# Attention beside a paged cache: the key banks' places in the order of steps are moved

## The reference

```python
def nsa_attend(q, qpos, kc, vc, ks_blk, vs_blk, kw, vw, kwpos, gate_logits, rel_bias):
    ...                                  # compressed branch: p_c, o_c, and the importance of each block
    top_val, top_idx = lax.top_k(score, min(TOP_BLOCKS, nb))
    k_sel = gather(ks_blk, top_idx)
    v_sel = gather(vs_blk, top_idx)
    ...
    s_s = einsum('bgrtd,..->bgrtj', qg, k_sel) * scale + bias_s
    p_s = masked_softmax(s_s, mask_s)
    o_s = einsum('bgrtj,..->btgrd', p_s, v_sel)
    ...
    s_w = jnp.einsum('btgrd,bsgd->bgrts', qg, kw) * scale + bias_w
    p_w = masked_softmax(s_w, mask_w)
    o_w = jnp.einsum('bgrts,bsgd->btgrd', p_w, vw)
    return (gts[:, :, 0] * o_c + gts[:, :, 1] * o_s + gts[:, :, 2] * o_w).reshape(b, t, NSA_Q)

def nsa_sample(x, cache_cmp, cache_slc, win_state, page_table, ...):
    ...
    fs = full_rows(cache_slc, kv_s)      # cache[page_table], with the new row behind it
    kw_all = jnp.concatenate([win_state, kv_w], axis=1)
    o = nsa_attend(q, qpos, kc, vc, ks_blk, vs_blk, kw_all[:, :, 0], kw_all[:, :, 1], kwpos, gl, rel_bias)
    return o @ w_out, kv_c, kv_s, kw_all[:, t:]
```

## Time and profile before

| | us |
|---|---|
| three runs | 1723.29, 1721.01, 1731.25 (median 1723.29) |
| the profiled execution | 1718.65 |
| its span, first to last instruction | 1717.0 |
| PE busy (matmul) | 1614.6, 94% |
| VectorE, ScalarE, GpSimd busy | 808.6, 551.0, 564.8 |
| attention, first score product to the last step's | 274.44 to 482.61 |

### The profile page before, as it was taken

How to read it: one execution, slowest core, us unless ns; L and a number is a source line. 1 busy time by engine, 2 the same in 40 slices (tenths; PEclk the granted TensorE clock), 3 DMA queues, 4 the chain that set the end, 5 groups by cost and what they waited for, 6 DMA issues and landing times. The chain is left out here.

```text
span 1717.0 us, 40632 instructions
## 1 busy us (share of the span) xinstructions
PE 1614.6 (94%) x16686; PEld 1502.3 (87%) x16686; DVE 808.6 (47%) x1350; ACT 551.0 (32%) x1040; POOL 564.8 (33%) x505
## 2 busy tenths in 40 slices
PE   6998997798989999999999899999989999999996
PEld 5998985555669999999999889989889999999995
DVE  4333114556555543444237676766447444343235
ACT  3110003456554322222235433333344222222242
POOL 0001222567633433443104333333014444343013
PEclk9999778899999999999999899999989999999998
DMA  9654687777752122223234234433221222223242
GB/s 285 211 187 178 217 293 276 287 239 228 218 193 79 59 88 87 97 86 119 89 132 145 83 113 96 141 111 100 75 89 60 76 96 86 97 86 118 94 160 84
DMA packets 86264, 238.50 MB, mean 139 GB/s; under 512 B 18109, under 2 KB 20847, under 8 KB 84545
## 3 DMA queue, kind: packets, MB, share of 16 engines
q1 hardware_dynamic: 80786, 221.63, 39.2%
q0 software_dynamic: 3392, 11.02, 1.8%
q10 hardware_dynamic: 1936, 3.74, 0.6%
HBM read 217.81 MB, written 23.77 MB: 141 GB/s over the span
## 5 line engine op out<-in xcount | busy, mean ns | idle before, releaser
L846 DVE TENSOR_TENSOR layer_w_lo<-ring,layer_w_hi 128x1024 fp32r<-128x1024 f32 (+1 forms) x138 | 225.5, 1634 | 265.8 <-ACT layer_w_hi L728 265.8
L993 PE MATMUL layer_ps<-layer_x_hi,layer_w_hi 128*128 128x260 f32 x1312 | 269.0, 284 | 2.7 <-DVE layer_w_lo L846 2.7
L993 PE MATMUL layer_ps<-layer_x_hi,layer_w_lo 128*128 128x260 f32 x1312 | 268.3, 284 | 0.0
L993 PE MATMUL layer_ps<-layer_x_lo,layer_w_hi 128*128 128x260 f32 x1312 | 267.8, 284 | 0.0
L728 ACT ACTIVATE layer_w_hi<-ring 128x1024 fp32r<-128x1024 f32 (+1 forms) x138 | 160.9, 1167 | 221.8 <-PE layer_ps L993 206.4
L993 PE MATMUL layer_ps<-layer_h_lo,layer_w_hi 128*128 128x260 f32 x960 | 217.6, 287 | 10.9 <-DVE layer_h_lo L852 10.9
L993 PEld LDWEIGHTS layer_ps<-layer_x_hi,layer_w_hi 128*128 128x128 f32 x1312 | 204.6, 189 | 4.3 <-DVE layer_w_lo L846 2.9
L993 PEld LDWEIGHTS layer_ps<-layer_x_hi,layer_w_lo 128*128 128x128 f32 x1312 | 204.7, 189 | 0.0
L993 PEld LDWEIGHTS layer_ps<-layer_x_lo,layer_w_hi 128*128 128x128 f32 x1312 | 204.0, 189 | 0.1
L993 PE MATMUL layer_ps<-layer_h_hi,layer_w_hi 128*128 128x260 f32 x704 | 172.8, 286 | 4.8 <-DVE layer_w_lo L846 4.8
L993 PEld LDWEIGHTS layer_ps<-layer_h_lo,layer_w_hi 128*128 128x128 f32 x960 | 160.8, 192 | 12.0 <-DVE layer_w_lo L846 11.8
(11 more groups left out here) (319 smaller groups left out, 3055.0 us busy)
## 6 DMA issues: line engine op xcount, KB each, us to landing
ring<-in_w_gu SPq DMA_DIRECT2D x88, 512.0 KB, 3.5
ring<-in_w_down SPq DMA_DIRECT2D x48, 704.0 KB, 4.1
arena<-in_cache_cmp SPq DMA_DIRECT2D x86, 256.0 KB, 5.1
ring<-in_hgrn_w_in SPq DMA_DIRECT2D x32, 512.0 KB, 3.7
X<-in_slc_kv SPq DMA_DIRECT2D x48, 256.0 KB, 3.3
ring<-in_nsa_w_in SPq DMA_DIRECT2D x21, 512.0 KB, 3.7
arena<-in_cache_cmp POOLq DMA_DIRECT2D x42, 256.0 KB, 5.5
ring<-in_slc_kv SPq DMA_DIRECT2D x40, 256.0 KB, 3.0
```

Of the source, the lines that this page charges most:

```text
L846: dve.tensor_tensor(self.w_lo[slot][:, 0:kcs * P], c.ring[:, s, 0:kcs * P], self.w_hi[slot][:, 0:kcs * P].bitcast(F32), ALU.subtract).then ...
L993: mm = pe.matmul(bank[:, h, 0:TH], wt[slot][:, a], xt[:, x, COLS[h]], start=start and part == 0, stop=stop and part == 2)
```

## The change

The four window banks get the turns 0, 3, 6 and 9. The first page bank gets 12 instead of 9, and the page banks follow each other by 2.2 steps instead of 2.45 before the rounding, which moves a turn away from steps of tile 3. The turns of the pages become 12, 15, 16, 18, 21, 24, 25, 27, 30, 31, 34, 36, 39, 40, 42, 45. Every operation of a bank moves with its turn; what the program does, and how often, stays.

```diff
 def bank_turns():
 
-    turns = [0, 1, 3, 6]
+    turns = [0, 3, 6, 9]
     for k in range(SLC_BANKS):
-        t = max(turns[-1] + 1, int(9 + 2.45 * k))
+        t = max(turns[-1] + 1, int(12 + 2.2 * k))
         turns.append(t + (t % 3 == 2))
     return turns
```

## The result

The changed kernel takes 1738.94 us (median of 15 runs, 1730.16 to 1743.56) where the kernel before takes 1723.29 (15 runs too): a ratio of 1.0088, with a 95% interval of 1.0070 to 1.0106. It is slower by 15.65 us. The forecast was +9.5.

The account below looks back on a forecast made before the run. It took TensorE, busy 94% of the span, as the bound, with attention running alone. Attention's first two parts -10.8, third +21.3, end -1.0 make +9.5 us: 1732.8 from a median of 1723.29, range 1713 to 1745.

Parts of the forecast that it names:

- third rival: Attention's early steps: no clock comes back and bank 3 stays 3 us late, so 5 us less gain: 1738; chance 0.1.
- steps 0 to 10: Early attention: less bank work, no window bank waits, one mix wait fewer and some clock back; -14.3 us.
- steps 11 to 19: Attention's second part: PE waits for bank 6, then bank 7 follows late, giving back +3.5 us.
- steps 20 to 46: Late attention: denser steps, nine page banks waited for (18.55 us) and 3.4 of clock; +21.3 us.
- from step 47 on: Attention's end: bank 18's mix leaves step 47, -1.0 us; the rest comes where it came.
- Bank 6's wait: Step 17: PE waits 4 to 5 us for bank 6, whose load stands behind the save of window 3.
- part 3: Attention's steps 20 to 46, 110.85 us before, predicted 132.15, with 3.4 for the clock.
- the nine named: Page banks 8, 10 to 13, 15 and 17 to 19 in steps 20 to 46: waits of 18.55 us in sum.
- The time from mix to scores: Page bank loads: from the mix that frees a slot until the new bank's scores can start, 11.75 us (11.3 to 12.5).
- the loads keep up: Rival: PE finds every page bank of steps 20 to 46 in time, -12.4 us, 1711 on the median's scale; chance 0.2.
- issue loop plus 2.7 for the last transfer: Page bank loads: SP issues eight transfers one by one in 8.02 to 9.06 us; the last lands about 2.7 later.
- Of the clock: Rival: all nine waits of steps 20 to 46 drop the clock, 1.7 us each, +11.9: 1745; chance 0.15.

Follow-up runs that it names:

- Experiment 4: The changed kernel with the window banks back at turns 0, 1, 3, 6 and the page banks as changed: 1745.89 us, ratio 1.0136.
- after: The profiled execution of the changed kernel, with no further edit against it: 1741.56 us.
- Experiments 2: The kernel before the change, with SP reading a bank's eight page numbers before it waits for the slot: 1714.02 us, ratio 0.9949.
- experiment 6: The changed kernel with page numbers read ahead and only the key half of every page transferred: 1711.31 us, ratio 0.9935.
- experiment 7: The changed kernel with window 3 saved earlier and page numbers read ahead, for two banks at once where loads follow closely: 1715.86 us, ratio 0.9974.

## Why the prediction was right, and where its sum was off

The direction, the mechanism and the range held; the sum, +9.5 for +15.65, fell short by 6. The total alone wouldn't have shown the mechanism: 1738.94 is nearer to the 1738 of the prediction's third rival, no early gain, than to the forecast's 1732.8. The steps and the experiments decide. By steps, each number less the 1.16 by which attention starts later in the second profile:

| | predicted | measured |
|---|---|---|
| steps 0 to 10 | -14.3 | -15.7 |
| steps 11 to 19 | +3.5 | +7.6 |
| steps 20 to 46 | +21.3 | +23.3 |
| from step 47 on | -1.0 | +0.2 |
| sum | +9.5 | +15.4 |

- **Steps 0 to 10, right.** Window banks 1 to 3 come without a wait; step 11 starts at 319.0 (320.4 predicted), and the clock rose (0.82 to 0.93 over steps 0 to 12); how much of the gain is the clock wasn't taken apart. Experiment 4 shows the gain by its absence: step 11 starts 59.95 after attention's start in its profile, 44.57 in after.
- **Steps 11 to 19, the step whose size was off most.** Bank 6's wait is 5.25 (4 to 5), in step 17 as said. But bank 7's scores come at 358.4, not 357.2, since bank 6's load starts 18.1 behind bank 5's (338.35 - 320.21) instead of 17.3, bank 7's 9.2 behind bank 6's instead of 8.8, and bank 7 lands in 12.07 instead of 10.7, though bank 5's load left 1.4 earlier than said; and the step takes 5.3 from there (359.58 to 364.87) instead of 3.8, because PE came out of the waits at the lower clock, 0.79 in step 19. The prediction carried the clock's price for part 3 only. Step 20 starts at 363.7 instead of 361.0, and step 11 had started 1.4 early: 4.1 in all.
- **Steps 20 to 46, nearly right.** Banks 8, 10 to 13, 15 and 17 to 19 wait, the nine named, for 1.52, 2.35, 2.22, 1.70, 4.00, 1.33, 2.00, 0.47 and 1.08: 16.7 where 18.55 were said. The time from mix to scores, 11.75 in the prediction (11.9 if the rows that it names are added up), was 11.5 to 11.9 for the four banks whose load nothing else held up, 8, 12, 15 and 19. Those held up by SP scattered more: bank 10 waited 2.35 where 1.1 was said, bank 18 0.47 where 2.3 was. The clock cost 1.8, 2.5 and 1.5 in steps 28, 32 and 41, 5.8 for 3.4. The remaining 1.4 is what the walk of PE's steps came out short by; it wasn't taken apart. So of the 23.3 that this part lost, 12.5 are more waiting (16.7 for 4.2), 4.0 more clock (5.8 for 1.8), and 6.8 the denser steps themselves, for which the prediction had 5.4. Experiments 2 and 6 show that share nearly without late loads: the part takes 104.88 with the old turns and no wait, 115.82 with the new ones and 2.9 of waits, 8.0 more.
- **The end, wrong.** Bank 18's mix leaves step 47, but step 48 then waits 1.61 for VectorE's copy. The prediction had that effect in its own list of steps, a longer step behind an empty one, and did not apply it here.
- **The rivals.** That the loads keep up would have given 1711, and experiment 6 measured 1711.31. That they agree so closely is luck: by steps it gained 16.5 up to step 19, where the rival had 10.8 with bank 6 still late, and lost 5.0 in steps 20 to 46, where the rival gained 0.6. Its argument came from the Trainium skill (DMA: Bandwidth & Descriptors, Issuing engines are not separate DMA queues), by which the time to initiate a transfer is usually small beside the transfer itself. The runs here don't agree: issuing took 8.0 to 8.6 of 11.1 us, and still 3.9 to 5.1 of 9.6 with the numbers read ahead. Cutting it by 4 us moved the landing by 1.7 only, so most of SP's time did lie beside the transfers; but even then a bank took 8.9 to 10.8, not the estimated 4.8. The prediction's own account, issue loop plus 2.7 for the last transfer, describes the loads as they were and misses what a shorter loop does: it would give 6.6 with a loop of 3.9. Of the clock, five of the eleven waits cost 1.5 to 2.5 us each, neither none nor all. That the early steps win nothing is refuted by the first row of the table and by experiment 4.

On the median's scale the steps' 5.9 us more make 1732.8 + 5.9 = 1738.7, beside 1738.94. What stays open is why a bank whose transfers are all issued within 4 us needs 9 to 11 for its 2.1 MB; other shapes of transfer, or other queues, weren't tried.

## What to carry to other kernels

When consumers of a ring of buffers are moved, walk for each buffer the steps from its release to its next use and set them against a measured landing; count what stands ahead on the issuing queue, and price the clock behind every wait. The two halves of such a change can each lose alone and don't add, so run each by itself. Here the order and the loads had to be changed together: reading addresses ahead gave 9.2 us, other turns alone nothing, both with an earlier save 19.4.

## What the runs showed that was not expected

- The landing of a bank follows its issuing only in part: 11.1 us behind the first transfer in the mean with loops of 8.0 to 8.6 us, 9.6 with loops of 3.9 to 5.1, and 6.0 and 7.8 for the two banks waited for with half the bytes and loops of 3.9 and 4.9. Where two loads overlapped in experiment 7, the second took 11.1 and 12.1 (318 GB/s in the window of the first pair).
- The clock can fall after a wait through which it held. Windows of experiment 7: the three after bank 10's wait of 2.67 us, its scores first (columns as above):

```profile
385.68:386.76 1.08, 1.08 (x33) 0.88 (x34) 0.03 (x1) 0.00 (x0) 1.08 (x2) 0.99 0.64 142
386.76:390.06 3.30, 3.30 (x21) 2.64 (x21) 0.96 (x3) 1.16 (x4) 0.63 (x1) 0.50 0.97 333
390.06:393.00 2.94, 2.94 (x35) 2.27 (x35) 1.74 (x11) 1.38 (x7) 0.20 (x1) 0.98 0.40 152
```

The scores ran at 2.4 GHz, then came 3.3 us of work at 1.2 GHz, then 2.4 again: 1.65 us lost. In the longer waits of after it fell before their end. The window of bank 6's wait:

```profile
344.00:349.32 5.32, 0.07 (x3) 0.00 (x1) 2.42 (x8) 1.52 (x4) 2.50 (x2) 0.71 0.77 223
```

Its scores right behind, 1.94 us long, had 0.50 throughout; bank 13's wait of 4.00 had 0.80, and its scores 0.50. In after the wait of 1.97 in step 19 was followed by a step at 0.79 and the longer one of 2.35 in step 26 by none, so the length of the wait alone doesn't decide; what does stays open here.
